# Layer norms by pairs of tiles, and extra products on TensorE, in a two-block transformer kernel

## The reference

```python
h = layer_norm(x)
for l in range(2):
    u = h * (1.0 + sc1) + sh1
    y = mixer(u, ...)          # mLSTM branch and dilated attention
    h = layer_norm(DN_ALPHA * h + g1 * y, ln1_g[l], ln1_b[l])
    u = h * (1.0 + sc2) + sh2
    y = swiglu(u, w1[l], w3[l], w2[l])
    h = layer_norm(DN_ALPHA * h + g2 * y, ln2_g[l], ln2_b[l])

def layer_norm(x, g, b):
    mu = x.mean(-1, keepdims=True)
    var = jnp.square(x - mu).mean(-1, keepdims=True)
    return (x - mu) * lax.rsqrt(var + LN_EPS) * g + b
```

## Time and profile before

| | |
|---|---|
| time, median of 3 runs | 2146.05 us (2141.42 to 2154.63) |
| profiled execution, its own time | 2150.18 us |
| its span, first to last instruction | 2148.4 us |
| TensorE products busy | 2018.0 us, 94% |
| VectorE busy | 1465.1 us, 68% |
| ScalarE busy | 1048.7 us, 49% |
| mean granted clock of TensorE | 0.980 |
| DMA | 358.98 MB, mean 167 GB/s |

### The profile page before, as it was taken

How to read it: one execution, slowest core, us unless ns; L and a number is a source line. 1 busy time by engine, 2 the same in 40 slices (tenths; PEclk the granted TensorE clock), 3 DMA queues, 4 the chain that set the end, 5 groups by cost and what they waited for, 6 DMA issues and landing times. The chain is left out here.

```text
span 2148.4 us, 37055 instructions
## 1 busy us (share of the span) xinstructions
PE 2018.0 (94%) x15578; PEld 1894.6 (88%) x15578; DVE 1465.1 (68%) x2624; ACT 1048.7 (49%) x1563; POOL 22.1 (1%) x36
## 2 busy tenths in 40 slices
PE   5999999989999999999999988999999989998998
PEld 4998888989999988899899978787999987888998
DVE  7787676677658877666675558875666578756665
ACT  3663454444445643554444434555555445555554
POOL 1000000000001000000000000000000000000000
PEclk8999999999999999999999999999999999999999
DMA  8545434547754555345465534222455343224552
GB/s 323 182 177 196 177 120 172 181 167 289 258 188 156 187 191 191 124 154 177 158 239 193 190 135 143 98 99 79 164 197 192 122 141 115 99 79 138 196 192 104
DMA packets 52770, 358.98 MB, mean 167 GB/s; under 512 B 5995, under 2 KB 8651, under 8 KB 9980
## 3 DMA queue, kind: packets, MB, share of 16 engines
q1 hardware_dynamic: 52476, 356.54, 46.8%
q10 hardware_dynamic: 128, 0.07, 0.0%
HBM read 355.41 MB, written 1.08 MB: 166 GB/s over the span
## 5 line engine op out<-in xcount | busy, mean ns | idle before, releaser
L353 DVE TENSOR_TENSOR w_lo<-raw,w_hi 128x1024 fp32r<-128x1024 f32 x340 | 409.6, 1226 | 242.8 <-ACT w_hi L673 241.4
L673 ACT ACTIVATE w_hi<-raw 128x1024 fp32r<-128x1024 f32 x338 | 349.9, 1054 | 346.2 <-PE projected L433 291.8
L433 PE MATMUL projected<-u_hi,w_hi 128*128 128x256 f32 x1728 | 490.3, 284 | 28.2 <-DVE u_lo L879 25.4
L433 PE MATMUL projected<-u_lo,w_hi 128*128 128x256 f32 x1728 | 483.7, 280 | 0.0
L433 PE MATMUL projected<-u_hi,w_lo 128*128 128x256 f32 x1728 | 483.6, 280 | 0.0
L433 PEld LDWEIGHTS projected<-u_hi,w_hi 128*128 128x128 f32 x1728 | 328.9, 190 | 35.9 <-issue 35.1
L1381 DVE TENSOR_TENSOR w_lo<-raw,w_hi 128x1024 fp32r<-128x1024 f32 x204 | 246.0, 1223 | 158.6 <-ACT w_hi L1710 158.6
L433 PEld LDWEIGHTS projected<-u_hi,w_lo 128*128 128x128 f32 x1728 | 327.7, 190 | 0.0
L433 PEld LDWEIGHTS projected<-u_lo,w_hi 128*128 128x128 f32 x1728 | 326.7, 189 | 0.2
L1443 PE MATMUL projected<-u_hi,w_hi 128*128 128x256 f32 x992 | 281.1, 283 | 18.5 <-DVE w_lo L1381 11.4
L1443 PE MATMUL projected<-u_lo,w_hi 128*128 128x256 f32 x992 | 278.6, 281 | 0.0
(11 more groups left out here) (371 smaller groups left out, 4055.2 us busy)
## 6 DMA issues: line engine op xcount, KB each, us to landing
raw<-in_stream_dram SPq DMA_DIRECT2D x324, 1024.0 KB, 4.9
w_mod<-in_first_ada_dram SPq DMA_DIRECT2D x8, 1024.0 KB, 15.3
band<-bias_rows SPq DMA_DIRECT2D x1, 3072.0 KB, 14.6
x<-in_xT_dram SPq DMA_DIRECT2D x1, 1024.0 KB, 5.0
out_dram<-uf SPq DMA_DIRECT2D x4, 256.0 KB, 2.5
tri<-in_tri_dram SPq DMA_DIRECT2D x2, 384.0 KB, 4.2
c<-in_c_dram SPq DMA_DIRECT2D x1, 512.0 KB
mask<-in_mask_dram SPq DMA_DIRECT2D x1, 384.0 KB, 25.5
```

Source lines behind the costliest of these rows:

```text
L353: eng.tensor_tensor(part(w_lo, step, half), raw_half(step, half), part(w_hi, step, half).bitcast(F32), ALU.subtract).then_inc(s_lo_dve, 1)
L433: m = pe.matmul(out, a, b, start=start and n == 0, stop=stop and n == 2, **kw)
L673: act.activation(part(w_hi, step, half), raw_half(step, half), ACT.Copy).then_inc(s_hi, 1)
```

## The change

Centring, squares and their sums in the four layer norms of block 1 go by pairs of tiles instead of halves of four. Two helpers add products whose results nobody reads: `keep_busy` (products of the identity with itself, float32, 128 columns each) and `turn_idle` (transposes of the identity). They write PSUM banks that are free at that place or that the next product overwrites.

```diff
+def keep_busy(pe, out, ident, count):
+    for _ in range(count):
+        pe.matmul(out[:, 0:P], ident[:], ident[:], start=True, stop=True)
+
+def turn_idle(pe, out, ident, count):
+    for b in range(count):
+        pe.transpose(out[:, b * P:(b + 1) * P], ident[:], ident[:])
...
             elif kind == "v":
+                if i == 0:
+                    turn_idle(pe, bank(step), ident, 4)
                 project_tokens(step, (u_hi, u_lo))
...
             elif kind == "ml_values":
+                keep_busy(pe, MB[0], ident, 7 if i else 4)
                 pe.wait_ge(s_mw, N + 1)
...
             elif kind == "wa":
                 pe.wait_ge(s_hn, l + 1)
+                if i == 0:
+                    turn_idle(pe, bank(step), ident, 4)
                 project(step, (hm_hi, hm_lo))
...
                 sum_features(l, i, 6).then_inc(s_mean, 1)
+                keep_busy(pe, MB[3], ident, 4)
                 for kt in range(KT):
-                    if kt % 4 == 0:
-                        pe.wait_ge(s_sq, 2 * N + kt // 4 + 1)
+                    if kt % 2 == 0:
+                        pe.wait_ge(s_sq, 4 * N + kt // 2 + 1)
                     m = pe.matmul(NB[i][1][:, 0:T], ones_d[:], sq[:, kt, :], start=kt == 0, stop=kt == KT - 1)
                 m.then_inc(s_var, 1)
+                keep_busy(pe, MB[3], ident, 8)
...
             elif kind == "w2":
                 pe.wait_ge(s_hid, N + 1)
+                if i == 0:
+                    turn_idle(pe, MB[3], ident, 4)
...
-                for n in range(2):
-                    act.wait_ge(s_cen, 2 * N + n + 1)
-                    act.activation(sq[:, 4 * n:4 * n + 4, :], cen[:, 4 * n:4 * n + 4, :], ACT.Square)\
+                for n in range(4):
+                    act.wait_ge(s_cen, 4 * N + n + 1)
+                    act.activation(sq[:, 2 * n:2 * n + 2, :], cen[:, 2 * n:2 * n + 2, :], ACT.Square)\
                        .then_inc(s_sq, 1)
...
-                for n in range(2):
-                    part = slice(4 * n, 4 * n + 4)
-                    mean = NB[i][0][:, 0:T].rearrange("p (o t) -> p o t", o=1).to_broadcast([P, 4, T])
+                for n in range(4):
+                    part = slice(2 * n, 2 * n + 2)
+                    mean = NB[i][0][:, 0:T].rearrange("p (o t) -> p o t", o=1).to_broadcast([P, 2, T])
                     dve.tensor_tensor(cen[:, part, :], hT[:, part, :], mean, ALU.subtract).then_inc(s_cen, 1)
-                dve.wait_ge(s_cen, 2 * N + 2)
+                dve.wait_ge(s_cen, 4 * N + 4)
...
             elif kind in ("wg", "wu"):      # block 2
+                if kind == "wu" and i == 0:
+                    turn_idle(pe, bank(step), ident, 4)
                 project(step, (u_hi, u_lo))
```

## The result

Over 20 executions of each on the same chips, the changed kernel took 2137.95 us in the median (2124.24 to 2146.30) and the kernel before 2150.43 (2138.12 to 2159.53). The ratio is 0.9942, 95% interval 0.9925 to 0.9959: 0.6% faster, where 0.9932 was forecast (2131.5 us against 2146.05). The profiled execution took 2137.07 us, span 2135.2, mean granted clock 0.986. "Fills" are the identity products of `keep_busy`, "turns" the transposes of `turn_idle`, and a "drop" is a stretch in which the granted clock is 0.50.

A forecast was written before the change was run, and what follows sets the result against it. TensorE, busy 94% of the span, was taken to bound the kernel, with time lost in waits and half-clock stretches; 3.9 + 6.5 + 7.2 - 3.0 = 14.6 us gained gave a median of 2132 us, range 2120 to 2147.

The forecast's parts named there:

- Pairs: In block 1's four layer norms the sums of squares start 0.97 us earlier each: 3.9 us gained.
- Norm fills: Identity products fit the norms' waits; no drops on three norms' sums and block 2's opening sum: 6.5 us gained.
- Fills before `ml_values`: 4 or 7 identity products before `ml_values` remove five drops of 1.43 us: 7.2 us gained, bounds 3.4 to 8.2.
- the drop at 779.8: Block 1 drop after no wait, behind products with four active rows; it lengthened its stretch by only 0.68 us.
- Turns: Four transposes at eight places: free at `w2` 0, 0.5 us at six others, 3.0 us lost, earning nothing.
- No wait under 2 us is followed by a drop: Block 1's trace: nine drops followed waits of 2.20 to 2.83 us, none followed waits of 1.24 or 1.35.
- The sum: Whole kernel: 3.9 + 6.5 + 7.2 - 3.0 = 14.6 us gained.
- Rival A: Identity products do nothing for the clock: only 0.9 us gained, median 2145 us; chance 0.17.
- Rival B: Identity products at 1.2 GHz stick out of their waits by 11.4 us: 10.5 us slower, median 2157; chance 0.07.
- rival C: Waits absorb turns at `v`, `wa`, `wu` 0 and drops are worth more: 5 us or so extra, median 2126; chance 0.21.
- The gap rule: Skill page: only TensorE idle gaps over about 3 us matter, so filling these waits would earn nothing for the clock.

The follow-up runs named there:

- doubled fills: Changed kernel without turns, with twice the identity products before `ml_values` and in the norms: 2141.90 us, ratio 0.9965 to the kernel before.
- one product at `wa`: Changed kernel with turns at `wa` 0 only, those four transposes replaced by one identity product: 2133.87 us, ratio 0.9943 to the kernel before.

## Why the prediction was right

**Pairs.** 0.97 us per norm were forecast; 2.47 - 1.51 = 0.96 measured, and from centring to next product 10.46 - 0.97 - 1.69 = 7.80 against 7.81. The two nearest rows of 128x512 carried over: a centring of two tiles took 0.68 us and a square 0.63.

**Norm fills.** They fit, as forecast (1.05 and 1.95 us in the waits). That no drop stands at the norms with them was right, 0 of 40 against 10 of 16. The term of 6.5 us was too large all the same: it took the drops of one execution, on three norms' sums and on block 2's first, for those of every execution. Turns alone had none on the three norms' sums, nor had the two kernels with pairs and without norm fills on any of eight, and behind a norm a drop costs 0.4 us at most. What the fills earn there in an average execution isn't measured.

**Fills before `ml_values`.** 7.2 us forecast, 8.8 in the profile, of which 0.9 is the drop at 779.8; the 7 products left waits of 0.63 to 1.06 us. All drops behind the waits before `ml_values` went: they stood behind 11 of 24 in the three profiles without fills, behind none of 88 in the eleven with. Drop for drop 1.43 us was right (27.55 to 26.10, 27.79 to 26.33). The first profile's five were more than the others had, though, which was three each.

**Turns.** Forecast 3.0 us lost. At `v` 0 they cost 0.5 us (the first `ml_values` comes at 159.2 us in the mean of four profiles, at 158.7 in eight without; left out are the doubled fills and pairs alone, which had a drop at 146.9), at `w2` 0 nothing, and at `wa` 0 they gain 0.9 per layer; at `wu` 0 no run prices them. The step failed in its sentence that they earn nothing; I had priced the instructions and not what a new start does to the stream behind. By these prices the four places at `v` 0 and `wa` 0 gain 0.8 us, where 2.0 lost were forecast. In sum the turns alone measured 0.9982 (0.9953 to 1.0011), from 10 us gained to 2.4 lost; that leaves 3.0 lost just outside, but with the two slowest of twelve left out, so this ratio alone doesn't settle it.

**Drops.** "No wait under 2 us is followed by a drop" held for block 1 in the one execution. After the change one fell at 711.5 behind a wait of 1.81 us and one at 885.6 behind a wait of 1.76 in attention; in the table they are part of the +4.9 us. In other profiles drops stand behind attention's waits of 1.40 us too. They don't make up for those that the fills take away: drops of block 1 that are neither at a norm nor behind `ml_values` number 1, 2 and 4 in the three profiles without fills and 2.3 in the mean of the ten with all of them.

And the drop at 779.8, behind products with four active rows and no wait, wasn't a stray. The fourteen profiles have fourteen such drops, in eleven of them. Each began 3.0 to 3.4 us after the first of the four products of L556 (L570 below), 1.6 to 2.0 after the last, with no idle time of TensorE over 0.1 us in between; no fill stands there. The changed kernel's second profile has one:

```profile
194.21 1.98 PE L570 MATMUL mixed<-rows,ident 4*128 4x512 f32 x4
...
197.40:200.80 3.40, 3.40 (x19) 3.40 (x18) 1.91 (x6) 1.53 (x4) 0.00 (x0) 0.50 0.46 195
```

**The sum.** 14.6 us forecast, 12.5 measured (2150.43 - 2137.95); pairs alone some 10, fills alone some 14, both without turns 15, by their ratios, each give or take 5. That 10 and 14 don't add up to 15 lies within that. The median is near the forecast partly by luck: 6.5 us for the norms' drops was too much, and so on average was 7.2 for those at `ml_values`, while of the 3.0 us taken off for the turns 2.0 stood at places that gained 0.8. The profiled pair's own 13.2 us agree with the forecast by luck too, since -12.4 and +13.2 us of spacing cancelled. With only one of these two one profile of each kernel would have shown about 0 or 26.

Rival A is out: fills alone measured 0.9934, the granted clock rose from 0.980 to 0.986, and the drops went from behind the waits before `ml_values`. Rival B's 11.4 us was high but of the right size (double fills at full clock take about as long as single ones at half, and cost 7.5 to 8.5 us), but the clock is full at the fills and its condition doesn't arise. Of rival C's extra a part came at `wa`, by the spacing and not by a wait that the turns shorten.

Of the versions run, the changed kernel with turns at `wa` 0 alone, without those at `wu` 0, and with those at `wa` 0 and `w2` 0 alone has the lowest ratios, 0.9888 (0.9852 to 0.9925), 0.9904 (0.9869 to 0.9939) and 0.9906 (0.9876 to 0.9935). The changed kernel itself measured 0.9942 and, once more, 0.9914 (0.9888 to 0.9940), so a lead over it isn't settled.

## What to carry to other kernels

Fill a wait of about 2 us on a bound TensorE with products that nobody reads only up to the length of the wait at full clock: measure the wait and leave a half microsecond. Splitting the work ahead of a wait is worth what it shortens it by (0.97 us a norm here), but it did not keep the clock up: with pairs alone the mean granted clock stayed at 0.981. Price a drop by where it falls: 1.4 to 1.7 us on a stream that bounds the kernel, next to nothing on products that wait for another engine anyway. And take the number of drops from several executions, not from one trace. Before you read a gain out of two profiles, compare the count of products in long undisturbed stretches; 4% there can be a state of the stream and not your edit, and a second profile of the same kernel shows which. With differences of 1% or less, a profile of the same kernel again is worth as much as one of a variant.

## What the runs showed of the hardware

A stream of split 256-column products runs at 113.4 or at 117.8 ns each at the same granted clock of 1.00, holds it for up to 1570 products, and may take the other at the next start. Four long feed-forwards with 6 to 7 us of difference each could account for most of the 12 to 33 us between the fastest and the slowest execution of one kernel. The profiles bear this out. Among the kernels with pairs and both kinds of single fill the span was 2119.9 us with no feed-forward at 117.8 ns (no turns at `wu`) and 2119.8 with one (turns at `wa` alone), 2133.8 to 2135.3 with two (changed kernel, `wa` and `w2`, one product at `wa`), and 2143.9 and 2144.6 with all four (no turns, the changed kernel again), some 6 us for each. Cutting block 1's streams into ten shows nothing more: that kernel's executions lay within 13 us, but so did those with a single product at `wa` and those without turns.

In block 1, past its opening, the granted clock fell to 0.50 for 3.4 us behind waits of 1.40 to 2.83 us, and not behind each of them, and fourteen times behind products with four active rows and no wait. The gap rule that the prediction quoted from the Trainium skill ("TensorE: Matmul & The Clock Gate", "Why this matters for your kernels"), no gaps over about 3 us, doesn't cover this kernel: with it the fills alone, which stand in waits of 1.24 to 2.83 us, would have gained nothing, and they measured 0.9934 at a mean granted clock of 0.986 instead of 0.980.
